# Moving one weight block's remainder, a pair's transposes and the places of the weight blocks in a transformer kernel

## The chip, the cores and the metric

The kernel runs on one core of a Trainium2 chip. Time is device microseconds (us) of one execution. Engines are named as the profile names them: PE (TensorE, its matmuls), PEld (the loads of stationary operands into PE), DVE (VectorE), ACT (ScalarE), POOL (GpSimd) and SP (SyncE, which here only issues DMAs).

## The reference

The input is one sequence of 512 tokens of width 1024, in float32. Two blocks follow one another.

```python
def first_block(x, ...):
    h = rmsnorm(x, norm_mix_pre)
    m = mixer(h, w_in, b_f, conv_w, w_branch, w_out)   # gated conv + 8-head attention
    x = x + rmsnorm(m, norm_mix_post)
    h = rmsnorm(x, norm_ffn_pre)
    g, u = split(h @ w_gate_up)                        # w_gate_up: 1024 x 2*2816
    return x + rmsnorm((silu(g) * u) @ w_down, norm_ffn_post)

def second_block(x, ...):                              # 16 heads, two score maps each
    h = rms_norm(x, norm_g)
    q, k, v, z = split(h @ w_in, 4)
    q, k = rms_norm(q) * 64 ** -0.5, rms_norm(k)       # per head and map
    probs = softmax(q @ k.T - slope * distance, causal)
    weights = probs[map 0] - lam * probs[map 1]
    o = rms_norm(weights @ v, head_norm_g) * (1 - lam_0) * silu(z)
    return x + o @ w_out
```

## The kernel before

Every product of float32 numbers is made of three matmuls on a high and a low part: ACT copies the raw value into a high part (`whi`, rounded to fp32r), DVE (or POOL) subtracts to get the low part (`wlo`), and PE adds high x high, high x low and low x high. In this text the low part of a weight block is called its remainder. A list of steps, written by the class `Order`, sets one order of work; each engine walks this same list and issues its own share of every step, so a step that stands earlier in the list comes earlier on every engine that takes part in it. Nothing is scheduled at run time, and an engine whose next instruction waits keeps all that is behind it waiting.

**The seven-product stage.** The gate and up projections of the feed-forward part are ten repetitions (j = 1 to 10) of a product of 2x2 blocks, done with seven block products (p = 0 to 6) in place of eight. A block product is 24 matmuls with a moving operand of 256 columns (step `gp`, lines 1162, 1164, 1165 of the profile). The moving operands are the activations (`hth`, `htl`) and sums of them (`sh`, `sl`). The stationary operands are weight blocks: three are parts of the raw weights (`raw`), four are sums `T1` to `T4` that POOL forms (step `wt`, line 2081, into `ts`). The step `ws(j, p)` splits block p: ACT copies it (line 1291) into its place in `whi`, DVE subtracts (line 1609) into the same place in `wlo`. There are four places of 1024 columns in `whi` and in `wlo`, and they begin `SHIFT` columns into the tensor; the ordinary half-slots of the other stages begin at column 0 and 2048. A column is 4 bytes. The step `gx(j, p)` combines the products out of PSUM: after product 3 DVE makes U2 and U3 (lines 1879 and 1881), after product 4 C22 (line 1885), each of which waits for the one ahead of it. PE's product 6 adds to a bank that C22 reads, and so waits for C22 as well as for the remainder of block 6. Products are counted from 0, as in the code.

**The pairs.** The second block's attention is written as seven pairs of heads (even, odd), `pair(even)`, each merged step by step with the projections of the next pair. The steps that matter, by head h: `t2(h, i)`, three groups of transposes of the weights `px`; ACT copies a group out of PSUM (`pth`, line 1291), DVE makes its low part (`ptl`, line 1609). `p2(h)`, the product with v (lines 1243 to 1245), in four parts of 512, 384, 256 and 128 columns; the third part needs group 2. `to(h)`: PE transposes the gate `og` (line 1261), DVE multiplies the head's output with it (`ots`, line 1985), and ACT waits for this and then issues the DMA that sends it to DRAM (line 1585). A bank of PSUM is drawn for each group from a ring of spare ones by `bank()`.

```python
        if past:
            put("to", even - 1, bank())
        put("t2", even, 2, bank())
        put("cb", odd, 2)
        yield
        put("p2", even, bank())
```

Of the kernel before, what the change touches and what calls it, by code (L numbers as in the profile page):

```python
# [172 lines left out]
class Order:  # L173
# [27 lines left out]
    def put(self, *step):  # L201
        self.steps.append(step)
# [42 lines left out]
    def bank(self):  # L245
        self.turns += 1
        return self.spare[self.turns % len(self.spare)]
# [195 lines left out]
    def gate_up(self):  # L443
        for p, a, t in [(p, a, t) for p in range(2) for t in range(4) for a in range(2)]:
            yield from self.unit(self.W.mix + a, 32, 4, "gu", p, a, t)
            if a == 1 and p == 1:
                self.put("guo", t)
            yield
        self.put("ws", 1, 2)
        self.put("hl", 0, 2)  # L450
        self.put("ws", 1, 3)
        self.put("hl", 3, 3)
        self.put("wt", 1, 3)
        for j in range(1, LASTJ + 1):
            for p in range(7):
                for q in range(4):
                    self.put("gp", j, p, q)
                    yield
                if j == LASTJ and p == 6:
                    self.split(self.W.dn, 4)  # L460
                self.put("gx", j, p)
                if p < 3:
                    if (j, p) != (1, 2):
                        self.put("ws", j, p + 4)
                elif j == 1 and p == 3:
                    self.put("ws", 1, 6)
                elif j == 1 and p == 4:
                    for i in range(2):
                        self.put("wt", 2, i)
                        self.put("ws", 2, i)  # L470
                elif j < LASTJ and p == 3:
                    self.put("wt", j + 1, 0)
                elif j < LASTJ:
                    if p == 4:
                        self.put("ws", j + 1, 0)
                    self.put("wt", j + 1, p - 3)
                    self.put("ws", j + 1, p - 3)
                elif p == 3:
                    self.owners[-1] = ("gp", j, 4, 3)
                    self.owners.append(("gp", j, 6, 3))  # L480
                    self.put("gs", 16)
                elif p == 4:
                    self.put("gs", 18)
                    self.split(self.W.dn, 2)
# [75 lines left out]
    def pair(self, even):  # L560
        put, bank, odd, past = self.put, self.bank, even + 1, even > 0
        self.scores(even, 0)
        self.scores(even, 1)
        yield
        if past:
            put("t2", even - 1, 0, bank())
        put("cb", even, 0)
        put("ab", odd)
        yield
        if past:  # L570
            self.second_tiles(even - 1)
            put("t2", even - 1, 2, bank())
        put("cb", even, 1)
        yield
        self.scores(even, 2)
        self.scores(odd, 0)
        yield
        put("cb", even, 2)
        yield
        if past:  # L580
            put("to", even - 2, bank())
        put("cb", even, 3)
        yield
        put("cb", odd, 0)
        put("ab", odd + 1)
        yield
        if past:
            put("p2", even - 1, bank())
        put("cb", odd, 1)
        yield  # L590
        put("t2", even, 0, bank())
        yield
        self.second_tiles(even)
        yield
        self.scores(odd, 1)
        self.scores(odd, 2)
        yield
        if past:
            put("to", even - 1, bank())
        put("t2", even, 2, bank())  # L600
        put("cb", odd, 2)
        yield
        put("p2", even, bank())
        put("cb", odd, 3)
        yield
        yield
# [35 lines left out]
def build(nc, A, out, x1_d, x2_d, ot_d):  # L642
# [10 lines left out]
    with ExitStack() as ctx:  # L653
# [194 lines left out]
        BANK = lambda j, p: RING[(5 * (j - 1) + BANKS[p]) % 8]  # L848
        first_slot = 2 * (1 - H[W.mix + 1].slot)
        assert first_slot == 0  # L850
        SHIFT = 80
        p1_t, sg0_t, u2_t, u3_t, c22_t, c21_t = (tf[0][:, 0:512], tf[0][:, 512:1024], tf[1][:, 0:512],
                                                 tf[1][:, 512:1024], xf[0][:, 0:512], xf[0][:, 512:1024])
        moving = [(lambda k: (hth[:, k, 0:256], htl[:, k, 0:256])), (lambda k: (sh[2][:, k, :], sl[2][:, k, :])),
# [6 lines left out]
        def slot_of(j, p):  # L861
            s = (first_slot + BLOCK(j, p)) % 4
            c = SHIFT + 1024 * ((s + 2) % 4)
            cs = slice(c, c + 1024)
# [740 lines left out]
        def _(e):  # L1605
# [32 lines left out]
            for s in STEPS:  # L1638
# [234 lines left out]
                elif kind == "gx":  # L1873
                    j, p = a
                    o = ps[BANK(j, p)][:, :]
                    if p == 3:
                        dve.wait_ge(snap_a, j)
                        dve.wait_ge(mm, PRODUCT(j, 3))
                        e.tensor_tensor(u2_t, o, p1_t, ALU.add).then_inc(comb_d, 1)
                        dve.wait_ge(comb_d, COMB(j, U2))  # L1880
                        e.tensor_tensor(u3_t, ps[BANK(j, 1)][:, :], u2_t, ALU.add).then_inc(comb_d, 1)
                    elif p == 4:
                        dve.wait_ge(comb_d, COMB(j, U3))
                        dve.wait_ge(mm, PRODUCT(j, 4))
                        e.tensor_tensor(c22_t, o, u3_t, ALU.add).then_inc(comb_d, 1)
                    elif p == 5:
                        dve.wait_ge(mm, PRODUCT(j, 5))
                        e.tensor_tensor(c21_t, u3_t, o, ALU.subtract).then_inc(comb_d, 1)
                    elif p == 6:
                        dve.wait_ge(sg1_a, j)  # L1890
                        dve.wait_ge(comb_d, COMB(j, C22))
                        e.tensor_tensor(gu[:, 2 * j:2 * j + 2, 256:512], pair(c21_t), pair(c22_t),
                                        ALU.mult).then_inc(comb_d, 1)
                        dve.wait_ge(mm, PRODUCT(j, 6))
                        e.tensor_tensor(u2_t, o, u2_t, ALU.add).then_inc(comb_d, 1)
                        dve.wait_ge(comb_d, COMB(j, C12))
                        dve.wait_ge(sg0_a, j)
                        e.tensor_tensor(gu[:, 2 * j:2 * j + 2, 0:256], pair(sg0_t), pair(u2_t),
                                        ALU.mult).then_inc(comb_d, 1)
# [293 lines left out]
```

## Time and profile before

| what | value |
|---|---|
| median of three runs | 1282.76 us (1282.42 to 1284.1) |
| the profiled execution: its own time | 1282.49 us |
| its span, from the first to the last instruction | 1280.8 us |
| time outside the span | 1.7 us |
| PE busy | 1274.0 us (99%) |
| PEld busy | 1085.6 us (85%) |
| DVE, ACT, POOL busy | 795.0, 611.6, 298.4 us |
| granted TensorE clock | 1.000 |

A matmul's busy time runs from its start to a modelled end, and matmuls overlap, so the busy time of one is longer than the time until the next one starts. Where matmuls follow one another without a wait, the length of a stretch over their number is the time that one of them costs. PE's idle time is the time in which none is under way; a wait that is shorter than the overlap shows less idle time than it costs.

### The profile page before, as it was taken

What the parts mean: (1) busy time and instruction counts of PE and PEld (TensorE: products, weight loads), DVE (VectorE), ACT (ScalarE), POOL (GpSimd) and SP (SyncE); (2) the same over time, 40 slices, a digit from 0 to 9 for tenths busy, and PEclk for the clock granted to TensorE, in tenths of its full rate; (3) what the DMA queues carried; (4) which work ended last, traced back from release to release, by engine and by line L of the source; (5) the groups of instructions that cost most, each with busy time, mean ns of one, the idle gap of its engine ahead of it and who ended that gap; (6) DMA issues with size and microseconds to landing.
All of it is one profiled execution on the core that took longest, in us unless ns stands there. A gap on an engine that the chain in (4) does not pass through costs nothing.

```text
span 1280.8 us, 18355 instructions
## 1 busy us (share of the span) xinstructions
PE 1274.0 (99%) x7170; PEld 1085.6 (85%) x7170; DVE 795.0 (62%) x1578; ACT 611.6 (48%) x1300; POOL 298.4 (23%) x203
## 2 busy tenths in 40 slices
PE   9999999999999999999999999999999999999999
PEld 6788888888899999999888888888888888887787
DVE  5435665443479987877333647676767667677743
ACT  5336654333445444445233445565556555556531
POOL 2023310000055656540001412131312223131110
PEclk9999999999999999999999999999999999999999
DMA  6322232333533334243226322222222222223511
GB/s 235 108 58 75 59 99 71 96 98 99 205 124 105 105 121 132 67 132 115 82 99 218 112 66 84 82 74 74 83 71 98 88 75 75 74 81 123 184 59 66
DMA packets 110441, 130.35 MB, mean 102 GB/s; under 512 B 7569, under 2 KB 87697, under 8 KB 110354
## 3 DMA queue, kind: packets, MB, share of 16 engines
q1 hardware_dynamic: 104594, 112.39, 27.2%
q10 hardware_dynamic: 5760, 16.78, 3.6%
q8 instruction: 57, 0.93, 0.3%
q14 instruction: 30, 0.25, 0.1%
HBM read 119.72 MB, written 9.44 MB: 101 GB/s over the span
## 4 chain that ended last, share of the span: by engine, by line
PE 98%; DVE 1%; ACT 0%; DMA 0%; POOL 0%; issue 0%; SPq 0%; ACTq 0%
PE ps L927 17%; PE ps L929 16%; PE ps L928 16%; PE ps L932 7%; PE ps L934 7%; PE ps L933 7%; PE ps L1164 5%; PE ps L1165 5%; PE ps L1162 5%; PE ps L1220 3%; PE ps L1230 1%; PE ps L1202 1%; PE ps L1254 1%; PE ps L1244 1%; PE ps L1245 1%; PE ps L1243 1%
## 5 line engine op out<-in xcount | busy, mean ns | idle before, releaser
L1609 DVE TENSOR_TENSOR wlo<-raw,whi 128x512 fp32r<-128x512 f32 (+1 forms) x294 | 233.7, 821 | 187.2 <-ACT whi L1291 186.5
L1291 ACT ACTIVATE whi<-raw 128x512 fp32r<-128x512 f32 (+2 forms) x338 | 208.5, 649 | 117.9 <-PE ps L929 84.5
L927 PE MATMUL ps<-whi,hth 128*128 128x512 f32 x592 | 242.3, 409 | 0.2 <-DVE wlo L1609 0.2
L929 PE MATMUL ps<-wlo,hth 128*128 128x512 f32 x592 | 231.5, 391 | 0.0
L928 PE MATMUL ps<-whi,htl 128*128 128x512 f32 x592 | 231.2, 390 | 0.0
L2043 POOL TENSOR_TENSOR wlo<-raw,whi 128x384 fp32r<-128x384 f32 (+1 forms) x44 | 49.2, 1135 | 416.6 <-ACT whi L1291 416.6
L927 PEld LDWEIGHTS ps<-whi,hth 128*128 128x128 f32 x592 | 111.3, 188 | 26.4 <-issue 5.2
L929 PEld LDWEIGHTS ps<-wlo,hth 128*128 128x128 f32 x592 | 111.1, 188 | 24.7
L928 PEld LDWEIGHTS ps<-whi,htl 128*128 128x128 f32 x592 | 111.6, 188 | 19.2
L932 PE MATMUL ps<-hth,whi 128*128 128x512 f32 (+1 forms) x288 | 111.5, 387 | 0.0
L934 PE MATMUL ps<-hth,wlo 128*128 128x512 f32 (+1 forms) x288 | 108.9, 378 | 0.0
L933 PE MATMUL ps<-htl,whi 128*128 128x512 f32 (+1 forms) x288 | 108.9, 378 | 0.0
L1559 ACT ACTIVATE px<-px,nm 128x128 f32<-128x128 f32 (+3 forms) x128 | 70.4, 551 | 54.4 <-DVE nm L1949 54.4
L1165 PE MATMUL ps<-sh,wlo 128*128 128x256 f32 x320 | 89.9, 281 | 0.0
L1162 PE MATMUL ps<-sh,whi 128*128 128x256 f32 x320 | 89.9, 281 | 0.0
L1164 PE MATMUL ps<-sl,whi 128*128 128x256 f32 x320 | 89.9, 281 | 0.0
L2012 POOL TENSOR_TENSOR rq<-rq,neghalf 128x8 f32<-128x8 f32 x32 | 52.4, 1638 | 123.1 <-DVE rq L1912 123.1
L2102 POOL TENSOR_TENSOR hn<-hn,neghalf 128x4 f32<-128x4 f32 x16 | 16.8, 1051 | 247.5 <-DVE hn L1976 247.5
L1291 ACT ACTIVATE px<-px,rl 128x128 f32<-128x128 f32 (+1 forms) x64 | 36.0, 562 | 78.8 <-DVE rl L1962 78.8
L1609 DVE TENSOR_TENSOR wlo<-ts,whi 128x1024 fp32r<-128x1024 f32 x40 | 66.5, 1684 | 4.1 <-ACT whi L1291 4.1
L2081 POOL TENSOR_TENSOR ts<-raw 128x1024 f32<-128x1024 f32 x20 | 58.3, 2916 | 40.0 <-DVE wlo L1609 38.6
L1162 PE MATMUL ps<-hth,whi 128*128 128x256 f32 x240 | 67.4, 281 | 0.0
(362 smaller groups left out, 2913.9 us busy)
## 6 DMA issues: line engine op xcount, KB each, us to landing
raw<-in_l_w_in SPq DMA_DIRECT2D x64, 512.0 KB, 4.4
raw<-in_w_gate_up SPq DMA_DIRECT2D x44, 512.0 KB, 4.7
raw<-in_w_in SPq DMA_DIRECT2D x13, 1024.0 KB, 5.2
raw<-in_w_down SPq DMA_DIRECT2D x10, 1024.0 KB, 4.9
raw<-in_l_w_out SPq DMA_DIRECT2D x8, 1024.0 KB, 5.0
raw<-in_w_in SPq DMA_DIRECT2D x26, 256.0 KB, 3.5
raw<-in_w_branch SPq DMA_DIRECT2D x8, 512.0 KB, 3.9
raw<-in_w_out SPq DMA_DIRECT2D x4, 1024.0 KB, 4.9
```

Of the source, the lines that this page charges most:

```text
L927: e.matmul(o, ah, wh[:, cs], start=a, stop=False)
L928: e.matmul(o, al, wh[:, cs], start=False, stop=False)
L929: m = e.matmul(o, ah, wl[:, cs], start=False, stop=z)
L932: e.matmul(o, wh[:, cs], ah, start=a, stop=False)
L933: e.matmul(o, wh[:, cs], al, start=False, stop=False)
L934: m = e.matmul(o, wl[:, cs], ah, start=False, stop=z)
L1162: e.matmul(o, wh[:, cs], ah, start=q == 0 and kt == 0 and p not in (2, 6), stop=False, skip_group_check=True)
L1164: e.matmul(o, wh[:, cs], al, start=False, stop=False, skip_group_check=True)
L1165: m = e.matmul(o, wl[:, cs], ah, start=False, stop=z, skip_group_check=True)
L1291: return e.activation(out, in_, ACT.Copy, **how)
L1559: e.activation(sl, sl, ACT.Exp, bias=nm2[:, c:c + 1], scale=-1.0, accum_out=ls2[:, c:c + 1]).then_inc(exp2_a, 1)
L1609: return e.tensor_tensor(out, src, hi_part.bitcast(F32), ALU.subtract)
```

## The change

There are three edits.

```diff
@@ gate_up: in repetition 1, ws(1, 6) goes from behind gx(1, 3) to behind gx(1, 2)
                 self.put("gx", j, p)
                 if p < 3:
-                    if (j, p) != (1, 2):
-                        self.put("ws", j, p + 4)
+                    self.put("ws", j, p + 4)
                 elif j == 1 and p == 3:
-                    self.put("ws", 1, 6)
+                    pass
@@ pair
         if past:
+            put("t2", even, 2, bank())
             put("to", even - 1, bank())
-        put("t2", even, 2, bank())
+        else:
+            put("t2", even, 2, bank())
@@ build
-        SHIFT = 80
+        SHIFT = 64
```

The four places of weight blocks begin 256 bytes into `whi` and `wlo`, where they began 320 bytes in. Nothing else about them changes: not their number, not the order in which they are used.

In the first repetition DVE's subtraction for block 6 (the one from `raw0`) stands ahead of U2 and U3. This is DVE's order around it before. `tf1` takes U2 and then U3, `xf0` takes C22, `wlo<-ts` are the remainders of blocks 4 and 5.

```order
L1609 TENSOR_TENSOR wlo<-ts2,whi 128x1024 [waits blk_hi]
L1609 TENSOR_TENSOR wlo<-ts0,whi 128x1024 [waits blk_hi]
L1879 TENSOR_TENSOR tf1<-ps6,tf0 128x512 [waits mm,snap_a]
L1881 TENSOR_TENSOR tf1<-ps3,tf1 128x512 [waits comb_d]
L1609 TENSOR_TENSOR wlo<-raw0,whi 128x1024 [waits blk_hi]
L1885 TENSOR_TENSOR xf0<-ps7,tf1 128x512 [waits mm,comb_d]
```

And this is the same place of the changed kernel.

```order
L1610 TENSOR_TENSOR wlo<-ts2,whi 128x1024 [waits blk_hi]
L1610 TENSOR_TENSOR wlo<-ts0,whi 128x1024 [waits blk_hi]
L1610 TENSOR_TENSOR wlo<-raw0,whi 128x1024 [waits blk_hi]
L1880 TENSOR_TENSOR tf1<-ps6,tf0 128x512 [waits mm,snap_a]
L1882 TENSOR_TENSOR tf1<-ps3,tf1 128x512 [waits comb_d]
L1886 TENSOR_TENSOR xf0<-ps7,tf1 128x512 [waits mm,comb_d]
```

The remainder has moved two places up. ACT had its copy of block 6 in the same place of its own order already, and repetitions 2 to 10 have this order in both kernels. Nothing moves on ACT, POOL, SP or PE here.

In each pair that has a pair ahead of it (six of the seven) the transposes of `px` stand ahead of those of `og`, on every engine. This is ACT's order in the last pair before: `zs1` ends the step ahead, `px3` belongs to the step behind.

```order
L1291 ACTIVATE v2h1<-ps1 128x256 [waits mm]
L1551 ACTIVATE zs1<-ps1 128x256
L1585 DMA ot_dram<-ots1 128x512 [waits ot_d2]
L1291 ACTIVATE pth2<-ps7 128x384 [waits t2_pe]
L1291 ACTIVATE px3<-px3,rl2 128x384 [waits rec2_d]
```

And this is it in the changed kernel.

```order
L1292 ACTIVATE v2h1<-ps1 128x256 [waits mm]
L1552 ACTIVATE zs1<-ps1 128x256
L1292 ACTIVATE pth2<-ps5 128x384 [waits t2_pe]
L1586 DMA ot_dram<-ots1 128x512 [waits ot_d2]
L1292 ACTIVATE px3<-px3,rl2 128x384 [waits rec2_d]
```

The copy of the transposes has changed places with the sending, and with the wait for `ot_d2` that the sending carries. On PE the same two groups change places; this is the last pair before.

```order
L1261 MATMUL ps5<-ident,og 128x128 [waits og_p,max2_d]
L1261 MATMUL ps5<-ident,og 128x128 x3
L1230 MATMUL ps7<-ident,px0 128x128 [waits max2_d]
L1230 MATMUL ps7<-ident,px0 128x128 x2
L927 MATMUL ps2<-whi,hth 128x512
```

And this is PE's order in the changed kernel.

```order
L1231 MATMUL ps5<-ident,px0 128x128 [waits max2_d]
L1231 MATMUL ps5<-ident,px0 128x128 x2
L1262 MATMUL ps7<-ident,og 128x128 [waits og_p,max2_d]
L1262 MATMUL ps7<-ident,og 128x128 x3
L928 MATMUL ps2<-whi,hth 128x512
```

The banks stay in their order, so the two groups also change banks. DVE's subtraction for `ptl` likewise stands ahead of its product for `ots` now. SP's and POOL's orders are as they were.

## Rows read from the trace of the kernel before

**Rows 1.** The page: busy us, share of the span, instructions.

```profile
PE 1274.0 (99%) x7170; PEld 1085.6 (85%) x7170; DVE 795.0 (62%) x1578; ACT 611.6 (48%) x1300; POOL 298.4 (23%) x203
```

**Rows 2.** Waits of PE, the two longest: line, releaser: us, times, longest.

```profile
PE ps L957 <- DMA kh_f<-in_norm_mix_pre: 2.2, 1, 2.2
PE ps L1243 <- DVE ptl L1609: 0.9, 1, 0.9
...
```

**Rows 3.** Busy time by stretch, PE: stretch, us, busy (x matmuls), clock, DMA.

```profile
378.20:392.10 13.90, 13.90 (x118) 1.00 0.24 75
392.25:590.10 197.85, 197.85 (x1682) 1.00 0.34 107
```

**Rows 4.** Groups by line, PEld, 372.5 to 391.5 us (unshifted places).

```profile
L932 PEld LDWEIGHTS ps<-hth,whi 128*128 128x128 f32 x27 | 5.2, 192 | 0.0
```

**Rows 5.** Groups by line, PEld, whole span (the seven-product stage).

```profile
L1162 PEld LDWEIGHTS ps<-sh,whi 128*128 128x128 f32 x320 | 61.4, 192 | 0.0
L1165 PEld LDWEIGHTS ps<-sh,wlo 128*128 128x128 f32 x320 | 60.1, 188 | 0.0
```

**Rows 6.** Timeline of DVE, repetition 1: start, us, engine, line, operation.

```profile
399.85 4.56 DVE L1609 TENSOR_TENSOR wlo<-ts,whi 128x1024 fp32r<-128x1024 f32 x2
404.34 0.68 DVE L1879 TENSOR_TENSOR tf<-ps,tf 128x512 f32<-128x512 f32 x1
...
405.66 2.10 DVE L1609 TENSOR_TENSOR wlo<-raw,whi 128x1024 fp32r<-128x1024 f32 x1
407.69 0.68 DVE L1885 TENSOR_TENSOR xf<-ps,tf 128x512 f32<-128x512 f32 x1
...
411.02 1.21 DVE L1609 TENSOR_TENSOR wlo<-ts,whi 128x1024 fp32r<-128x1024 f32 x1
```

**Rows 7.** Timeline of POOL, repetition 1.

```profile
403.36 3.32 POOL L2081 TENSOR_TENSOR ts<-ts,raw 128x1024 f32<-128x1024 f32 x1 [1.16 <-DVE wlo L1609]
```

**Rows 8.** Timeline of PE: the start of product 6, repetition 1.

```profile
409.21 0.28 PE L1162 MATMUL ps<-sh,whi 128*128 128x256 f32 x1
```

**Rows 9.** Timeline of DVE, repetition 2.

```profile
423.27 3.42 DVE L1609 TENSOR_TENSOR wlo<-raw,whi 128x1024 fp32r<-128x1024 f32 x1
...
428.06 0.69 DVE L1885 TENSOR_TENSOR xf<-ps,tf 128x512 f32<-128x512 f32 x1
```

**Rows 10.** Timeline of POOL, repetition 2.

```profile
422.41 3.21 POOL L2081 TENSOR_TENSOR ts<-ts,raw 128x1024 f32<-128x1024 f32 x1
```

**Rows 11.** Timeline of PE, last pair: `p2`, its parts of 384 and 256 columns.

```profile
1164.78 0.34 PE L1244 MATMUL ps<-pth,v2l 128*128 128x384 f32 x1
1164.95 0.34 PE L1245 MATMUL ps<-ptl,v2h 128*128 128x384 f32 x1
1166.21 0.39 PE L1243 MATMUL ps<-pth,v2h 128*128 128x256 f32 x1 [0.92 <-DVE ptl L1609]
```

**Rows 12.** Timeline of ACT, last pair.

```profile
1162.72 0.36 ACT L1551 ACTIVATE zs<-ps 128x256 f32<-128x256 f32 x1
1164.71 0.33 ACTq L1585 DMA_DIRECT2D ot_dram<-ots  x1
1165.08 0.49 ACT L1291 ACTIVATE pth<-ps 128x384 fp32r<-128x384 f32 x1 [2.00 <-DVE ots L1985]
1166.52 0.61 ACT L1291 ACTIVATE px<-px,rl 128x384 f32<-128x384 f32 x1 [0.94 <-DVE rl L1962]
```

**Rows 13.** Timeline of DVE, last pair.

```profile
1163.61 0.41 DVE L1934 SCALAR_TENSOR_TENSOR zs<-zs,ps 128x256 f32<-128x256 f32 x1
1163.93 0.74 DVE L1985 SCALAR_TENSOR_TENSOR ots<-oc,gh,ps 128x512 f32<-128x512 f32 x1
1165.60 0.56 DVE L1609 TENSOR_TENSOR ptl<-ps,pth 128x384 fp32r<-128x384 f32 x1 [0.93 <-ACT pth L1291]
```

**Rows 14.** Timeline of all engines from 1184.5 us: the gate `og` of head 12.

```profile
1184.73 1.04 POOL L2105 TENSOR_TENSOR og<-zs,hn 128x512 f32<-128x512 f32 x1
...
1186.06 0.60 PE L1261 MATMUL ps<-ident,og 128*128 128x128 f32 x4
```

## The prediction

> **What bounds the kernel now.** I read the page first: PE is busy for 1274.0 us of the span, so 6.8 us are all that waits can give back [rows 1]. Next PE's own waits: apart from the start (2.2 us for the first data) one stands out, a wait of line 1243 for DVE's `ptl`, a single time, 0.9 us [rows 2]. The rest is under 1 us together. So the change can gain in two ways only: at this wait, or by making the matmuls themselves cheaper; and it loses wherever PE is made to wait anew. The matmuls' price is in the busy time by stretch: the seven-product stage lasts 197.85 us, and its count of 1682 holds the two or so that were under way when the stretch begins; its own 1680 cost 117.8 ns each, at full granted clock [rows 3].
>
> **Edit 1, the places (SHIFT 80 to 64).** It adds no instruction. What it could alter is the price of the 1680 matmuls. The trace has one comparison. Just ahead of the stage the same shape (256 moving columns, 128 stationary) runs from places that begin at byte 0 of a slot: 118 matmuls in 13.90 us, of which 2.4 were under way at its start (0.28 us of each by 0.12 between starts), so 120.2 ns each, 2.4 more [rows 3, 8]. The loads tell the same: there a load takes 192 ns, in the stage a third of them takes 192 and the others 188 [rows 4, 5]. So a start at byte 0 goes with slow loads throughout, and one at byte 320 with a slow third; 120.2 less 117.8 over two thirds is 3.6 ns for each load that is slow, about the 192 less 188. What byte 256 does no row shows. The bounds: all loads slow, 1120 more of them, about +3.7 us (1120 x 3.3, with the durations unrounded between 3.3 and 3.6); all fast, 560 fewer, -1.9 us. I take 0, the state of now: 256 is nearer to 320 than to 0, and nothing says that the effect turns between them.
> A rule of the Trainium skill would make it exactly 0: the page "TensorE: Matmul & The Clock Gate", section "Step-by-step: what each phase is for", says that the moving operand and the weight load have independent read ports in SBUF, so that the loading of the next weights takes nothing from the running matmul. The rows agree only in part, since 188 and 192 ns stand beside one another for one shape.
>
> **Edit 2, the remainder of block 6 ahead of U2 and U3 in repetition 1.** No instruction is added; one subtraction moves up past two on DVE. What is late next is C22. Now: DVE ends the remainder of block 5 at 404.41 (399.85 + 4.56), makes U2 from 404.34 (starts overlap by 0.07) and U3, starts block 6's remainder at 405.66, ends C22 at 407.69 + 0.68 = 408.37 [rows 6]. PE starts product 6 at 409.21 [rows 8], 0.84 us later, and this is the cover.
> How long does the subtraction take at its new place? Alone it takes 1.21 us, in its old place 2.10 [rows 6]. The difference is POOL: its addition begins at 403.36 and takes 3.32 us, to 406.68, and DVE's subtraction ends 1.08 us behind that, at 407.76 [rows 7, 6]. U2 and U3, which read PSUM, passed beside POOL at 0.68 us each. Put first, the subtraction starts at 404.34, in the midst of POOL's addition, and the waiting that U2 and U3 now fill is lost. Repetition 2 shows just this order under just this cover: POOL's addition begins at 422.41, takes 3.21, to 425.62; DVE's subtraction from `raw` begins at 423.27 and takes 3.42, to 426.69, again 1.07 behind POOL's end; U2, U3 and C22 follow, and C22 ends at 428.06 + 0.69 = 428.75, 5.48 us after the subtraction began [rows 9, 10]. In repetition 1 that gives 404.34 + 5.48 = 409.82 for C22, against PE's 409.21. PE waits 0.61 us, and some 0.04 more for the handover (as DVE's end to ACT's issue below): **+0.65 us**. If DVE came ahead of POOL, the subtraction would take 1.21 us, C22 would be ready near 408, and the cost is 0. I take +0.65, since repetition 2 shows the order itself. The remainder itself ends at 407.76 as before, so SP's load behind it does not start earlier.
> The page "SBUF — State Buffer" of the Trainium skill, section "Who interferes with whom", has the rule: DVE and GpSimd share one pair of ports, held by one for a whole instruction while the other is fully blocked. The trace agrees (the subtraction ends 1.08 and 1.07 us after POOL's, with 1.21 alone).
>
> **Edit 3, the transposes ahead of the sending.** PE does the same seven transposes in the other order: 0. In the last pair DVE multiplies `ots` from 1163.93 for 0.74 us, ACT issues the DMA at 1164.71 (0.04 after its end) and only then copies `pth`, at 1165.08, though its step before ended at 1163.08; DVE follows with `ptl` at 1165.60 for 0.56 [rows 12, 13]. PE's third part of `p2` starts at 1166.21. Its matmuls of 384 columns come 0.17 us apart, so it would have started at 1165.12: 1.09 us are lost there, of which 0.92 show as idle [rows 11]. With the order turned, ACT copies at about 1163.1 to 1163.6; DVE makes `ptl` when its step before ends (1163.61 + 0.41 = 1164.02), to 1164.6; PE asks at 1165.12. The wait is gone with 0.5 us to spare: **-1.09 us**. In the five other pairs the edit gives nothing, since [rows 2] has this wait once.
> What is late next: `ots` now starts near 1164.5 and the DMA issues near 1165.3, 0.6 later; behind it ACT's `px`, at 1166.52 now, waits for a DVE chain that had stood behind `ptl`; that moves up by about 0.95 (`ptl` and `ots`, 0.56 + 0.74, then follow 1164.02 without DVE's gap of 0.93). The tightest place behind is the gate of head 12: POOL has it ready at 1184.73 + 1.04 = 1185.77 and PE takes it at 1186.06 [rows 14], 0.29 us. If PE comes 1.09 earlier and the gate 0.95, 0.15 is left, and nothing is lost. If the gate did not move at all, PE would wait there, and only 0.29 of the 1.09 would stay.
>
> **The sum.** 0 + 0.65 - 1.09 = -0.44 us. Against the profiled execution's own time: 1282.49 - 0.44 = 1282.05. That execution lies 0.27 us under the median of three, so for a median I say 1282.76 - 0.44 = **1282.3 us**: no change that a measurement tells, whose bound I put at 0.2%, or 2.6 us.
>
> **The rivals.**
> (a) The places cost: at 256 bytes all loads take 192 ns as at 0. For it: 256 divides by more than 320 does, as 0 does. Against: the effect need not go by that. 1282.3 + 3.7 = 1286.0, slower. With half of that (two loads of three slow) it is +1.9, 1284.2. It decides, as slower by 0.2% with the other edits' -0.4, from about 900 more slow loads of 3.3 ns.
> (b) The places gain: the slow third of the loads goes too, -1.9, 1280.4. For it: the effect has more to give. The far end: 384 columns cost 0.17 us a matmul [rows 11], so 256 can't be shown to cost less than two thirds, 113 ns; 4.8 ns on 1680 is -8.1, 1274.2. No row comes near this for the shape, so I give it little.
> (c) The ports are kinder in repetition 1 than in 2 and edit 2 costs nothing: 1281.7. Against it stands repetition 2.
> (d) The gate of head 12 does not come forward: 1282.76 + 0.65 - 0.29 = 1283.1. For it: its margin is 0.29 us. Against: all the chain to it starts from the DVE work that moves up.
>
> **How the numbers follow.** My forecast 0.44; (c) 0.10; (d) 0.08; (a) in full 0.12, in part 0.07; (b) 0.14, its far end 0.05. The range goes from 1279.8 (b with c, 1280.4 - 0.6) to 1284.8 (a in part with the 0.8 that d adds, less the spread of the runs): it leaves out (a) in full and the far end of (b), 0.17. Faster by over 0.2% (under 1280.2): the far end, and most of (b), which lies 0.2 us off the bound, 0.16; slower (over 1285.3): (a) in full and a little of its part, 0.14; within: 0.70.
>
> **What would show it.** In the trace after: the stage's loads at 192, 188, 188 ns and its matmuls at 117.8 ns (if edit 1 is 0); in repetition 1 DVE's `wlo<-raw` of about 3.4 us from 404.34, C22's end at 409.8 and a wait of PE at line 1162 for DVE `xf`; no wait of line 1243 for `ptl`; the gate of head 12 ready some 0.15 us ahead of PE. The forecast is wrong if the stage's length leaves 197.85 us by over 1 us, for then the places decide and both other edits are small beside them.

## The result: slower by 0.2%, and the profile after

The changed kernel takes 1286.03 us in the median of 16 runs (1285.11 to 1286.93), the kernel before 1282.83 us (16 runs, 1281.69 to 1285.26). The ratio is 1.0023, 95% interval 1.0016 to 1.003. The forecast was 1282.3 with a range up to 1284.8. The rival (a), priced at 1286.0, is what came.

The page's busy times in the profiled execution after, to be read beside [rows 1]:

```profile
PE 1278.2 (100%) x7170; PEld 1090.3 (85%) x7170; DVE 789.7 (62%) x1578; ACT 612.0 (48%) x1300; POOL 297.8 (23%) x203
```

PE's waits, beside [rows 2] (line, releaser: us, times, longest):

```profile
PE ps L958 <- DMA kh_f<-in_norm_mix_pre: 2.3, 1, 2.3
PE ps L928 <- DVE wlo L1610: 0.2, 1, 0.2
PE ps L971 <- DVE sx L1662: 0.2, 1, 0.2
PE ps L1163 <- DVE xf L1886: 0.2, 1, 0.2
```

PE waits less than before, and the span is 3.1 us longer, so the matmuls themselves became dearer. The same two stretches as in [rows 3], the second also lengthened until it holds the stage (columns: stretch, us, then busy time and count of each engine):

```profile
378.30:392.10 13.80, 13.80 (x117) 13.80 (x116) 13.47 (x12) 6.78 (x9) 8.98 (x4) 1.00 0.25 74
392.25:590.10 197.85, 197.68 (x1648) 197.47 (x1647) 156.72 (x141) 91.15 (x103) 107.41 (x37) 1.00 0.34 107
392.25:593.90 201.65, 201.48 (x1680) 201.28 (x1678) 159.31 (x145) 92.50 (x106) 107.41 (x37) 1.00 0.33 105
```

In the 197.85 us that held 1682 matmuls before, 1648 start or run now, at the same full clock. And PE's weight loads in the stage, beside [rows 5]:

```profile
L1163 PEld LDWEIGHTS ps<-sh,whi 128*128 128x128 f32 x320 | 61.4, 192 | 0.4 <-DVE xf L1886 0.4
L1165 PEld LDWEIGHTS ps<-sl,whi 128*128 128x128 f32 x320 | 61.4, 192 | 0.0
L1166 PEld LDWEIGHTS ps<-sh,wlo 128*128 128x128 f32 x320 | 61.4, 192 | 0.0
```

All loads take 192 ns, as in the unshifted stretch ahead of the stage [rows 4]. Edits 2 and 3 can be read in the timeline: first DVE and POOL in repetition 1, then PE at product 6, then ACT and DVE in the last pair.

```profile
404.44 3.42 DVE L1610 TENSOR_TENSOR wlo<-raw,whi 128x1024 fp32r<-128x1024 f32 x1
...
409.22 0.69 DVE L1886 TENSOR_TENSOR xf<-ps,tf 128x512 f32<-128x512 f32 x1
...
403.45 3.32 POOL L2082 TENSOR_TENSOR ts<-ts,raw 128x1024 f32<-128x1024 f32 x1 [1.16 <-DVE wlo L1610]
...
409.51 0.28 PE L1166 MATMUL ps<-hth,wlo 128*128 128x256 f32 x1
409.96 0.39 PE L1163 MATMUL ps<-sh,whi 128*128 128x256 f32 x1 [0.17 <-DVE xf L1886]
...
1167.07 0.48 ACT L1292 ACTIVATE pth<-ps 128x384 fp32r<-128x384 f32 x1
1168.03 0.55 DVE L1610 TENSOR_TENSOR ptl<-ps,pth 128x384 fp32r<-128x384 f32 x1
...
1169.22 0.29 PE L1244 MATMUL ps<-pth,v2h 128*128 128x256 f32 x1
```

The subtraction takes 3.42 us at its new place and C22 ends at 409.91, as worked out ahead (3.4 and 409.82); the subtraction ends 1.09 behind POOL's addition, as in the two places read before. PE starts product 6 0.45 after the matmul ahead of it where 0.12 is usual: 0.33 lost. The second matmul then comes 0.22 behind the first (line 1165, at 410.18), which loses 0.10 more: 0.43 in all. In the last pair `ptl` is ready at 1168.58, and PE's third part starts at 1169.22 without a wait.

The account after: stage +3.7 (1680 matmuls 2.2 ns dearer), C22 +0.4, pair -1.1: +3.0, of the 3.1 and 3.2 that spans and medians differ by.

### The profile page after: what moved, and what is told of

The parts are those of the page before. It is cut to its first block, busy times and chain, and to the rows that moved or that the text cites. A ratio compares the mean times of both kernels' runs of the same rounds, so it can differ in the third digit from the quotient of the medians.

```text
span 1283.9 us, 18355 instructions
## 1 busy us (share of the span) xinstructions
PE 1278.2 (100%) x7170; PEld 1090.3 (85%) x7170; DVE 789.7 (62%) x1578; ACT 612.0 (48%) x1300; POOL 297.8 (23%) x203
## 4 chain that ended last, share of the span: by engine, by line
PE 96%; DVE 2%; DMA 0%; issue 0%; ACT 0%; POOL 0%; SPq 0%; DVEq 0%
PE ps L928 17%; PE ps L930 16%; PE ps L929 16%; PE ps L933 7%; PE ps L934 6%; PE ps L935 6%; PE ps L1163 5%; PE ps L1166 5%; PE ps L1165 5%; PE ps L1221 3%; PE ps L1231 1%; PE ps L1203 1%; DVE wlo L1610 1%; PE ps L1255 1%; PE ps L1246 1%; PE ps L1245 1%
## 5 line engine op out<-in xcount | busy, mean ns | idle before, releaser
L1610 DVE TENSOR_TENSOR wlo<-raw,whi 128x512 fp32r<-128x512 f32 (+1 forms) x294 | 229.8, 808 | 190.5 <-ACT whi L1292 189.8
L1165 PE MATMUL ps<-htl,whi 128*128 128x256 f32 x240 | 67.9, 283 | 0.0
```

The source lines that it names most:

```text
L1165: e.matmul(o, wh[:, cs], al, start=False, stop=False, skip_group_check=True)
L1610: return e.tensor_tensor(out, src, hi_part.bitcast(F32), ALU.subtract)
```

## The experiments

### Each edit alone

`e1_shift64` is the kernel before with `SHIFT = 64`.

> The kernel before with edit 1 alone (weight places 256 bytes in, where they were 320). If the places alone set the seven-product stage's price, this run has the loads at 192 ns on all three lines, matmuls 120.0 ns apart (117.8 before, 1680 of them, +3.8 us), no new wait of PE, and a time of about 1282.8 + 3.8 = 1286.6 us, so 0.6 above the changed kernel, which has the other two edits (-1.1 and +0.3) as well. Rival: the three edits need each other (the stage is slow only with the moved remainder); then the loads stay at 192, 188, 188 and the time at 1282.8.

Measured: 1286.55 us against 1282.92, ratio 1.0029 (1.0019 to 1.004), and no new wait. The stage's stretch, in the view of busy time by stretch (PE's count is the first):

```profile
392.25:590.10 197.85, 197.85 (x1651) 197.85 (x1650) 157.82 (x142) 91.20 (x103) 107.43 (x37) 1.00 0.33 107
```

1651 less the 2.4 under way at the start make 120.0 ns each, and all loads are at 192 ns. Edit 1 alone costs 3.6 us, more than the 3.2 of all three edits together: the number 64 in place of 80 is the whole of the loss, and the rival that the edits need each other is out.

`e2_ws` has edit 2 alone (the diff's first piece).

> The kernel before with edit 2 alone (block 6's remainder ahead of U2 and U3 in repetition 1). In the changed kernel the subtraction took 3.42 us from 404.44 and PE waited 0.33 us at 409.5, less than the 0.65 forecast. If the difference is that PE came later to product 6 there, since its matmuls had become dearer, then PE comes on time here and waits 0.6 to 0.7 us: C22 ready at 409.8, PE asking at 409.2, time 1283.4. Rival: the handover hides part of it whatever PE does, the wait is 0.3 again, time 1283.1. Neither can be told from no change by the times alone; the trace's wait tells them apart.

The profiled execution has PE waiting 0.5, and the start of product 6 comes 0.76 after the matmul ahead, 0.64 late:

```profile
409.58 0.28 PE L1164 MATMUL ps<-hth,wlo 128*128 128x256 f32 x1
410.34 0.39 PE L1161 MATMUL ps<-sh,whi 128*128 128x256 f32 x1 [0.48 <-DVE xf L1884]
```

So the first theory holds: the 0.65 was right for a PE that is on time. The second matmul behind the restart is late by another 0.10, as in the changed kernel, so the wait costs 0.74 in all. The times were a surprise: seven executions took 1282.9 to 1284.3, with a median 0.67 above the kernel before, and four took 1276.5 to 1277.2. The kernel before, in the 23 executions taken beside them, never left 1282.0 to 1284.4.

`e3_pair` has edit 3 alone.

> The kernel before with edit 3 alone (px's transposes ahead of og's in each pair). If the wait of the last pair goes and nothing takes its place: no wait of PE for ptl, time 1282.8 - 1.1 = 1281.7. Rival: the gate of head 12, or the second block's tail, takes back the gain once PE comes earlier, which the changed kernel with its later PE could not show; then PE waits for og near 1185, and the time is 1282.5 or above.

Measured: 1281.88 against 1282.92, no wait for `ptl`. The difference of 1.04 is the 1.09 of the forecast, though the interval of the ratio (0.9983 to 1.0001) does not exclude none; the wait's absence from the list is the firmer evidence. The gate of head 12 is ready 0.15 ahead of PE, as worked out:

```profile
1184.63 1.04 POOL L2107 TENSOR_TENSOR og<-zs,hn 128x512 f32<-128x512 f32 x1
1185.82 0.63 PE L1263 MATMUL ps<-ident,og 128*128 128x128 f32 x4
```

### Which offsets cost what

```diff
-        SHIFT = 80
+        OFFS = (0, 16, 32, 48)
-            c = SHIFT + 1024 * ((s + 2) % 4)
+            q = (s + 2) % 4
+            c = OFFS[q] + 1024 * q
```

`e4_map` is this kernel; `e5_map` has (80, 96, 112, 128). Successive products use successive places.

> The kernel before with the four weight places 0, 64, 128 and 192 bytes off a 512-byte step, one offset for each place, so that every product's 24 matmuls show the price of one offset. Theory A, what counts is an odd multiple of 64 bytes (320 is 5 x 64, 256 and 0 are even): the places at 64 and 192 run at 117.8 ns a matmul with two loads of three at 188, those at 0 and 128 at 120.0 with all loads at 192, and the time is half way, about 1282.8 + 1.9 = 1284.7. Theory B, what counts is that the start lies past the middle of a 512-byte step (320 does, 256 and 0 do not): all four places at 120.0, time 1286.6. Theory C, any place not a multiple of 256 bytes is cheap: three places of four cheap, 1283.7.

> The kernel before with the four places 320, 384, 448 and 512 bytes in (one offset for each place). The first such map gave 117.8 ns a matmul at 64 and at 192 bytes, 118.7 at 128 and 119.6 to 120.0 at 0. Theory A, the price goes by the offset's largest power of two and not by its size: 320 and 448 (odd multiples of 64) at 117.8, 384 (an odd multiple of 128) at 118.7, 512 at 120.0; stage shorter than with all at 256 by 1.8 us, time about 1284.4. Rival: it goes by the distance from the last 512-byte step, and 384 and 448 are cheap or dear whatever divides them; then 384 would be at 117.8 like 320.

The first matmul of five successive products, on PE's timeline of the first map:

```profile
406.95 0.28 PE L1163 MATMUL ps<-hth,whi 128*128 128x256 f32 x1
409.77 0.28 PE L1163 MATMUL ps<-sh,whi 128*128 128x256 f32 x1
412.64 0.28 PE L1163 MATMUL ps<-hth,whi 128*128 128x256 f32 x1
415.47 0.28 PE L1163 MATMUL ps<-sh,whi 128*128 128x256 f32 x1
418.32 0.28 PE L1163 MATMUL ps<-hth,whi 128*128 128x256 f32 x1
```

And of the second:

```profile
405.84 0.28 PE L1163 MATMUL ps<-hth,whi 128*128 128x256 f32 x1
408.71 0.28 PE L1163 MATMUL ps<-sh,whi 128*128 128x256 f32 x1
411.54 0.28 PE L1163 MATMUL ps<-hth,whi 128*128 128x256 f32 x1
414.39 0.28 PE L1163 MATMUL ps<-sh,whi 128*128 128x256 f32 x1
417.22 0.28 PE L1163 MATMUL ps<-hth,whi 128*128 128x256 f32 x1
```

A product is 24 matmuls, so the differences give for the places at 192, 0, 64 and 128 bytes 2.82, 2.87, 2.83 and 2.85 us (117.5, 119.6, 117.9, 118.8 ns a matmul), and for 512, 320, 384 and 448 bytes 2.87, 2.83, 2.85 and 2.83. Three levels come out: odd multiples of 64 bytes are cheap, odd multiples of 128 cost 1 ns more, multiples of 256 cost 2 ns more. None of the theories stated for the first map holds as it stands: A had the place at 128 at 120.0 and it came at 118.8, B had all four at 120.0, C had three cheap. Theory A as restated for the second map holds; the distance from a 512-byte step does not matter, and "256 is nearer to 320 than to 0" was no argument. The times, of one execution each, were 1284.24 and 1283.29. How long the loads take does not give the price by itself: at the place at 128 bytes they took 188 and 189 ns, no more than at the cheap ones, and a matmul cost 118.8.

`e9_pad` has the offsets of the first map and 64 bytes of padding in front of `hth`. `e15_pad64` has the padding and all four places at 64 bytes (`SHIFT = 16`).

```diff
+        sbuf(ctx, "pad", [P, 16])
         hth = sbuf(ctx, "hth", [P, KD, S], F32R)
```

> The four places at 0, 64, 128 and 192 bytes once more, with the moving operands of this stage (hth, htl, sh, sl) and all that lies behind them in SBUF moved up by 64 bytes. If the price goes by the weights' own address, the places keep their order: 64 and 192 at 117.8 ns, 128 at 118.7, 0 at 119.6. If it goes by where the weights lie against the moving operand, the place at 64 now stands as 0 did and becomes the dear one (119.6 or 120.0), 128 and 0 become cheap (117.8), and 192 costs 118.7.

> All four places at 64 bytes, and the moving operands (with all that lies behind them) 64 bytes up as well, so that weights and moving operand stand against each other as with 0 and 0. If only the distance between them counts: all matmuls of the stage 120.0 ns apart, all loads 192 ns. If the weights' own address counts: 117.8, since 64 is an odd multiple of 64. The whole is slow either way, near 1297, since 512-column matmuls took 233 ns in place of 227 in the other kernel with this padding.

Product starts on PE's timeline of `e9_pad`, places 64, 128, 192, 0 in turn:

```profile
414.85 0.28 PE L1164 MATMUL ps<-hth,whi 128*128 128x256 f32 x1
417.74 0.28 PE L1164 MATMUL ps<-sh,whi 128*128 128x256 f32 x1
420.46 0.28 PE L1164 MATMUL ps<-hth,whi 128*128 128x256 f32 x1
423.30 0.28 PE L1164 MATMUL ps<-sh,whi 128*128 128x256 f32 x1
426.13 0.28 PE L1164 MATMUL ps<-sh,whi 128*128 128x256 f32 x1
```

Busy time of `e15_pad64` in the stage:

```profile
395.00:590.00 195.00, 195.00 (x1627) 194.97 (x1626) 156.11 (x140) 89.95 (x101) 108.49 (x37) 1.00 0.33 105
```

And one of its groups of loads:

```profile
L1165 PEld LDWEIGHTS ps<-sl,whi 128*128 128x128 f32 x320 | 61.4, 192 | 0.0
```

The place at 64 bytes is now the dearest (2.89 us, 120.4 ns), 192 costs what 128 did (2.84, 118.3), 0 what 64 did (2.83, 117.9), and 128 falls to 2.72 us, 113.3 ns. With all at 64 and 64 it is 195.00 / (1627 - 2.4) = 120.0 ns and 192 ns for the loads, as with 0 and 0. So the dear place moves with the moving operand: it is where the weights lie against it that makes a place dear, not their own address. One thing the distance does not tell. The two kernels go through the same distances in the same order (0, 64, 128, 192 bytes, modulo 256), and 64 bytes behind the dear place a matmul costs 117.9 in the first map and 113.3 here, in 15 of 17 rounds (2.72 or 2.73 us a product) and without a wait or a cut. The next section looks at these two prices. The page "TensorE: Matmul & The Clock Gate" of the Trainium skill, section "Step-by-step: what each phase is for", which lets the two reads go through independent ports, does not cover this: by it all these kernels would have one price. They have not, and the measurement decides.

Both kernels with padding are slow as wholes (1296.63 and 1300.79 us), since the matmuls of 512 columns are shifted as well. Summed from start to start they take 14.7 and 14.9 us more than in the kernel before; those of line 929 with `guh`, for example, come 233 ns apart for 226. `e6_half` shows the same from the other side. It begins the ordinary half-slots 320 bytes in.

> The kernel before with the ordinary half-slots of whi and wlo 320 bytes in as well (they begin at 0 and 8192 bytes in the kernel before). The matmuls of 256 columns ahead of the seven-product stage (the gate and up projections of the first slice, and those fed by yah) should go from 120.0 to 117.8 ns apart, those of 64 to 96 matmuls some 0.2 us in all. For the 3000 matmuls of 512 columns there are two theories. If a start off the 256-byte step makes every weight load cheaper, they go from 227 to about 224.5 ns and the time falls by up to 7 us, to 1276. If only the spacing of short matmuls feels a load, nothing moves, and the time is 1282.6.

It took 1287.24 us, so the first theory fails, and with its sign turned. For example the matmuls of line 929 with `guh`, 389 ns each in the kernel before, take 394 (groups by line, PE; their starts lie 231 ns apart for 226), while their loads stay at 188:

```profile
L929 PE MATMUL ps<-wlo,guh 128*128 128x512 f32 x160 | 63.0, 394 | 0.0
```

The price of this shift is larger than the time shows. The seven-product stage, whose places this run leaves alone, changed its pace on the way (PE's busy time in two stretches of it):

```profile
398.85:434.00 35.15, 35.15 (x301) 1.00 0.28 91
438.35:588.00 149.65, 149.65 (x1323) 1.00 0.36 113
```

Each count less 2.4 gives 117.7 ns a matmul in the first and 113.3 in the second. The switch comes at the start of product 6 of repetition 2 (435.57), which C22 had let go only 0.13 us before (435.44), where the kernel before has 0.24. From start to start the matmuls of 512 columns take 10.6 us more than in the kernel before and those of 256 columns 6.5 us less. Some pairs of operands did not mind: `whi` with `guh` came 226 ns apart for 227. The matmuls of 256 columns right ahead of the stage went from 120.0 to 117.6 ns, as expected (67 counted in 7.60 us).

### A third pace

`e2_again` and `e7_two` looked for the executions of 1276.5 to 1277.2 us.

> Edit 2 alone once more, for a profile of the executions of 1276.5 to 1277.2 us, of which there were four in eleven. If this profile shows one: theory one, PE's stream of matmuls in the seven-product stage takes another pace after its wait at product 6, and 6.5 us over the 1530 matmuls behind it make 113.5 ns each in place of 117.8; theory two, the stage stays at 117.8 and the time is missing elsewhere. If it shows 1283.4, the matter stays open.

> The changed kernel without edit 1: places at 320 bytes, edits 2 and 3 made. If the edits add up: 1282.9 + 0.5 (PE's wait for C22, as with edit 2 alone) - 1.1 = 1282.3, which is what was forecast for all three. A rival is open from the run with edit 2 alone: four of its eleven executions took 1276.5 to 1277.2, 6.5 us less than the others. If that belongs to edit 2 at 320 bytes, some executions here fall to about 1275.5; if it was something of that one build or moment, none does.

The first gave 1284.08, nothing new. The second, edits 2 and 3 without edit 1, has ten executions in two groups: five of 1275.14 to 1275.76 and five of 1281.99 to 1283.93, and the profiled one is of the first. PE's timeline at its wait:

```profile
409.08 0.28 PE L1166 MATMUL ps<-hth,wlo 128*128 128x256 f32 x1
409.85 0.38 PE L1163 MATMUL ps<-sh,whi 128*128 128x256 f32 x1 [0.49 <-DVE xf L1886]
410.07 0.28 PE L1165 MATMUL ps<-sl,whi 128*128 128x256 f32 x1
410.18 0.28 PE L1166 MATMUL ps<-sh,wlo 128*128 128x256 f32 x1
410.29 0.28 PE L1163 MATMUL ps<-sh,whi 128*128 128x256 f32 x1
```

And its busy time in a stretch behind it:

```profile
411.25:583.25 172.00, 172.00 (x1520) 1.00 0.38 120
```

Ahead of the wait the products of 24 matmuls begin 2.83 us apart (117.8 ns a matmul) as in the kernel before, behind it 172.00 / (1520 - 2.4) = 113.3 ns, at once and to the end of the stage, over the same places. The loads of all three lines take 188 ns there, for example (groups by line in that stretch):

```profile
L1163 PEld LDWEIGHTS ps<-sh,whi 128*128 128x128 f32 x291 | 54.6, 188 | 0.0
```

So at 320 bytes the stream has two lasting paces, and a restart after a wait can move it to the lower one: it did in this trace, and did not in those of `e2_ws` and `e2_again`. `e11_kick80` and `e12_kick64` disturb it without a wait:

```diff
+        KICK = {(2, 0): (128,), (3, 0): (64,), (4, 0): (192,), (5, 0): (32,),
+                (6, 0): (224,), (7, 0): (16,), (8, 0): (240,), (9, 0): (64, 192)}
...
-                        e.matmul(o, wh[:, cs], ah, start=q == 0 and kt == 0 and p not in (2, 6), stop=False,
-                                 skip_group_check=True)
+                        cuts = KICK.get((j, p), ()) if (q, kt) == (1, 2) else ()
+                        for c0, c1 in zip((0,) + cuts, cuts + (256,)):
+                            e.matmul(o[:, c0:c1], wh[:, cs], ah[:, c0:c1],
+                                     start=q == 0 and kt == 0 and p not in (2, 6), stop=False,
+                                     skip_group_check=True)
```

> The kernel before (places at 320 bytes) with one matmul of 256 columns cut in two or three at one point of each of the repetitions 2 to 9: 128+128, 64+192, 192+64, 32+224, 224+32, 16+240, 240+16, 64+128+64 columns. The results are the same; what changes is PE's rhythm at that point, without a wait. In the profiled execution of edits 2 and 3 together the matmuls behind PE's wait at product 6 came 113.3 ns apart, in the other executions seen 117.8. Theory one: the addresses allow more than one lasting pace, and a disturbance of any kind can move the stream from one to the other; then some cuts here are followed by 113.3 ns to the next cut, and the time falls below 1282.8 by up to 6. Theory two: the pace of 113.3 comes from something else that the moved remainder brings (DVE's or POOL's timing); then all stretches stay at 117.8, and each cut costs 20 to 60 ns, time 1283.2.

> The same cuts with the places at 256 bytes. Theory one: at 256 bytes the lower pace does not exist, whatever disturbs the stream, as the 16 executions of the changed kernel have it (a wait at product 6, and all at 1285 to 1287); every stretch stays at 120.0, time about 1286.9. Theory two: the lower pace exists here as well, and the wait of the changed kernel only did not reach it; then some stretches run at 113.3 as with 320 bytes, and edit 1 costs nothing that a cut would not give back.

At 320 bytes (1279.08 us), the busy time ahead of the first cut, between it and the last, and behind the last:

```profile
392.70:412.50 19.80, 19.80 (x170) 19.80 (x169) 19.77 (x15) 10.06 (x11) 12.77 (x4) 1.00 0.15 49
413.90:547.00 133.10, 133.01 (x1173) 132.81 (x1172) 117.88 (x98) 62.25 (x71) 84.34 (x29) 1.00 0.38 120
548.30:586.00 37.70, 37.70 (x322) 37.70 (x321) 28.10 (x30) 17.18 (x22) 11.99 (x4) 1.00 0.27 94
```

And at 256 bytes (1287.05 us), the stage from end to end:

```profile
393.00:592.00 199.00, 199.00 (x1663) 199.00 (x1662) 156.57 (x143) 90.44 (x103) 106.40 (x37) 1.00 0.33 107
```

Each count less 2.4 gives at 320 bytes 118 ns, then 113.7 with six cuts and a delay in it (113.3 between them), then 118 again, since the cut in three parts leads back out. At 256 bytes it gives 119.8, the nine extra pieces being short: 120.0 between the cuts. The eight cuts here never led to a lower pace, nor did the wait at product 6 in the changed kernel, if it stands in all of its 16 executions as in the profiled one (none took under 1285.1). So theory one holds in both kernels.

`e13_onecut` takes edit 3, the places at 320 bytes and one cut of 128+128 in repetition 1 (`KICK = {(1, 0): (128,)}`); `e14_tencuts` such a cut in each repetition.

> Edit 3 alone, places at 320 bytes, and one cut of 128+128 columns in product 0 of repetition 1, near 393 us. If such a cut always moves the stream to 113.3 ns and the waits of PE behind it leave it there: 1660 matmuls x 4.5 ns = -7.4 us against edit 3 alone (1281.9), plus a wait or two of 0.3 to 0.6 at products 6 that a faster PE meets, so about 1275 in every execution. If it is chance, executions fall in two groups, near 1275 and near 1282.5, as with edit 2. If the lower pace is reached but lost at a wait, between: 1281.

> The same with such a cut in product 0 of each of the ten repetitions. If cuts of 128+128 always lead to 113.3 ns, from 117.8 as from 113.3, all executions are near 1275.2 (each cut costs about 0.02), also where a wait had lost the pace. If a cut can also lead out of 113.3 (the cut of 64+128+64 did), stretches of both paces alternate, and the time lies between 1276 and 1282.

`e13_onecut` took 1275.60 us (1275.42 to 1276.42, five runs) against 1282.58: ratio 0.9944, 0.9931 to 0.9956. Every execution is in the lower group, which edit 3 alone never reached in its eleven; this kernel beats both. Its busy time from the cut to the first small delay, and then in the stage:

```profile
395.70:404.40 8.70, 8.70 (x79) 1.00 0.01 3
395.70:582.00 186.30, 185.60 (x1636) 185.33 (x1635) 168.16 (x139) 88.54 (x102) 108.94 (x37) 1.00 0.36 114
```

And PE's timeline at its wait at product 6, in repetition 2 now:

```profile
430.03 0.38 PE L1167 MATMUL ps<-sh,whi 128*128 128x256 f32 x1 [0.69 <-DVE xf L1891]
430.25 0.29 PE L1170 MATMUL ps<-sl,whi 128*128 128x256 f32 x1
```

The first line gives 113.6 ns, so the lower pace begins at the cut, ahead of any wait; the second gives 114.0 ns a matmul with the wait in it. The faster stream runs into C22 of repetition 2, which the kernel before had ready only 0.2 us ahead of PE (at 428.75, [rows 9]), and keeps its pace past that wait. Against edit 3 alone (1281.88) the gain is some 6 us of the 7.4 that the pace promised; the wait (0.86 from start to start) and a delay of 0.17 at product 4 of repetition 1 take the rest. Ten cuts gave 1276.66 (1276.23 to 1277.36): no better than one. In its profiled execution the lower pace stands behind each of the ten cuts, so a cut of 128+128 does not lead out of it.

## Why the prediction was wrong, step by step

- **Edit 1, the step that failed.** The forecast took 0 between its bounds of -1.9 and +3.7, "256 is nearer to 320 than to 0, and nothing says that the effect turns between them". The effect does turn: it goes by what divides the offset (64, 128 or 256 bytes), and 256 counts as 0. The upper bound was the true price: 3.7 forecast for all loads slow, 3.6 measured with edit 1 alone (2.2 ns on each of 1680 matmuls). The row that told it was there, all loads 192 ns at byte 0 [rows 4]; what lacked was the thought that an address acts by its remainder and not by its size. Rival (a) had that thought and got 0.12.
- **The price of a slow load, a second flaw of the same step.** The forecast took 3.3 to 3.6 ns for each slow load and so -1.9 us for a stage without any. The upper bound came right, since it rests on matmuls measured at 120.2 ns. The lower one did not: where `e7_two` has all loads at 188 ns, a matmul costs 113.3, which is -7.6 us on 1680. And at 128 bytes the loads are at 188 and 189 with a matmul at 118.8. The loads' time goes along with the pace in some cases and is not its price.
- **Edit 2, right.** 0.65 forecast; in the run with edit 2 alone product 6 starts 0.64 late, and 0.74 are lost with the late second matmul, which the forecast did not have. In the changed kernel the start is 0.33 late (0.43 lost), since its dearer matmuls brought PE to product 6 later: 144 of them ahead at 2.2 ns each are 0.3 us. The two terms do not add.
- **Edit 3, right.** -1.09 forecast, -1.04 measured; margin of the gate of head 12 0.15 forecast and found, so rival (d) is out. Rival (c) is out: the subtraction took 3.42 us.
- **Rival (b), out for 256 bytes**, but its far end of 113 ns a matmul, "no row comes near this", exists: at 320 bytes, once the stream is disturbed. So the forecast missed that edit 2's wait would have brought some 7 us in nine of 22 executions, had edit 1 not been made. That the pace can change at the wait is shown by one trace with the switch at the wait; how often it does, by the times of the two kernels, in which the nine stand at least 5.7 us below the rest of their kernel.
- Left open: why the price goes by the distance, and why in two paces. That it is a conflict of two reads in SBUF is an inference from the dependence on their distance; no record shows it, and what decides the pace at a restart, or in the padded kernel at 64 bytes, was not found.

## What to carry to other kernels

Where PE is the bound, compare start-to-start times of one matmul shape across the program's places: 2 ns on 1680 matmuls was the whole result. Place weights and moving operands by the remainder of their distance, measured per shape: 256 columns wanted an odd multiple of 64 bytes, 512 columns, taken together, wanted none. When a run's time is used to price a shift, look at every stage of its trace: in `e6_half` a lucky pace in one stage hid 6 of the 10.6 us that the shift cost in the others. And when the executions of one kernel fall in two groups, look for a stream that locks into one of two paces, and for a small edit (here one cut matmul) that picks the better.

## What the hardware showed unexpectedly

- The price of a matmul of 256 columns by distance of weights and moving operand: 120.0 ns at 0 and 256 bytes, 118.3 to 118.8 at 128, 117.8 at odd multiples of 64, with a second pace of 113.3 there. In the padded kernel the place 64 bytes from the moving operand had 113.3 round after round, in the first map 117.9 at the same distance.
- One pace is kept over 1500 matmuls and four places. It fell in nine of the 22 executions with edit 2's wait at product 6, in one of `e6_half` at a product 6 that had no visible wait, and with a first cut of 128+128 columns in all eleven (five each of `e13_onecut` and `e14_tencuts`, a trace of each and the times of the others, and one of `e11_kick80` by its trace). A cut of 64+128+64 raised it again, once.
- A faster PE arrives earlier and finds the next wait: with 113.3 ns the cover of C22 in repetition 2 (0.2 us) became a wait of 0.69.
